# Moving the small projection's load to third place in each group of the gate's loads, and its products behind the group's first unit

## The chip, the cores and the metric

One core of a Trainium2 chip runs the kernel. The metric is the device time of one execution, in microseconds (us); the median of three runs is compared. A profile is one such execution, taken by the hardware profiler. Matrix products run on TensorE (PE; its weight loads are PEld), element-wise work on VectorE (DVE), ScalarE (ACT) and GpSimd (POOL), and SyncE (SP) issues the large weight loads from memory. Each engine works through its own program in order and meets the others at semaphores.

## The reference

Two transformer-like blocks in float32 follow each other on one sequence of 256 rows of 2048 values. The place that matters here is the end of the first block, after its MLP:

```python
        h = h + rms_norm(f, norm_mlp_post[i])
        h = h + jax.nn.sigmoid(h @ ple_gate[i]) * (p[i] @ ple_proj[i])
```

`ple_gate` is 2048 x 2048 (the gate) and `ple_proj` is 256 x 2048 (the small projection); `p` is 256 x 256. The result `h` then feeds the second block, whose first large product is with `w_in_2`.

## The kernel before, in words

**Units.** A weight matrix is read in column chunks of 512. A chunk of a 2048-row weight comes in four loads of 1 MB (rows 512 u to 512 u + 511, u = 0 to 3), each into one of four slots of the buffer `raw`. One such load with its products is a unit. For float32 accuracy the unit is split in two parts: ACT copies it to `whi` in fp32r (`hand_split`, L1112), DVE writes the rest, `raw - whi`, to `wlo` (`hand_low`, L1599), and PE then runs 24 matmuls of 128x512 for it, for two row halves b (`hand_unit`, L655 to L657). `whi` and `wlo` have two buffers each, so the split of a unit waits until PE is through with the unit two before it.

**The order of loads.** The first part of the program runs on one list that is written out by hand, `order` (L369 to L374), and turned into `HAND`. Entry n goes to slot n % 4. SP walks down that list and issues one load per entry (L535 to L558). Before load n it waits until entry n - 4, which lay in the same slot, has been used: for a split unit until DVE has written its `wlo` (`lo_ready`, L539), for a plain one, which PE reads straight from `raw`, until its products are done (`plain_used`, L541). SP is one queue: a load that waits holds up all loads behind it.

**The gate stage.** The gate has four chunks (i = 0 to 3) of four units (u = 0 to 3); the sixteen are the entries "gate". For each chunk there is one plain entry "pp" with the chunk's 512 columns of the small projection (0.5 MB, L547). Before the change each group of five entries reads pp, gate, gate, gate, gate. PE walks through the gate units (L912 to L927) and runs the chunk's small products behind unit u = 2: four float32 matmuls of 128x512 (L925), which the trace shows as eight. They write to PSUM banks 4 and 5 (even i) or 6 and 7 (odd i). Before them PE waits for the load (`raw_in`) and, for i of 2 and 3, for `gate_mul`, that is, for DVE to have read the bank's content of two chunks ago.

When a chunk's last unit is done, ACT takes the sigmoid of both halves (`sigmoids`, L1395), and DVE multiplies it with the small products (L2003, behind `plain_used`) and adds it to `h` (L2004, `gated`). ACT then forms row squares (L1345). After the last chunk DVE scales the rows, PE transposes them (L600, `turned("m2_00", ...)`), and the stage `in2_0` with 52 units begins (L931).

What sets the order around the change is therefore the list `order`, with the test in L916; nothing is scheduled by a program.

Of the kernel before, what the change touches and what calls it, by code (L numbers as in the profile page):

```python
# [91 lines left out]
def build(nc, I, out):  # L92
    ctx = ExitStack()
    with ctx:
# [261 lines left out]
        def laid(order):  # L356

            out_, done, s_, p_, a_ = [], {}, 0, 0, -2
            for r_, name in enumerate(order):
                ph = BY[name]  # L360
                k = done.get(name, 0)
                done[name] = k + 1
                if ph.split and k % UPC == 0:
                    a_ += 2
                out_.append(Unit(ph, k // UPC, k % UPC, r_, s_ if ph.split else None, None if ph.split else p_, a_))
                s_, p_ = s_ + (1 if ph.split else 0), p_ + (0 if ph.split else 1)
            return out_

        order = []  # L369
# [1 line left out]
            order += ["in1" if n < 36 else "in1g"] + (["mod0"] if n % 5 < 4 else [])  # L371
        order += ["in2_0c"] * 4 + ["cmp", "in2_0c"] * 4 + ["in2_0c"] * 40
        order += ["out1"] * 16 + ["in2_0c"] * 4 + ["mlp"] * 128
        order += (["pp"] + ["gate"] * 4) * 4 + ["in2_0"] * 52  # L374
        HAND = laid(order)
        SPLIT = [x for x in HAND if x.s is not None]

# [206 lines left out]
        def _(pe):  # L584
# [57 lines left out]
            def hand_unit(x, A):  # L642

                pe.wait_ge(lo_ready, x.s + 1)
                hi_, lo_ = A
                w = x.ph.width
                for b in range(TB):
                    a, bank = half(x, b)
                    if x.u == 0 and a >= 3:
                        pe.wait_ge(half_out, a - 2)  # L650
                    tt = slice(b * P, b * P + P)
                    dst = ps[:, bank, 0:w]
                    for k in range(UK):
                        kk = UK * x.u + k
                        mm(dst, hi_[:, kk, tt], whi[:, x.s % 2, k, 0:w], start=(kk == 0), stop=False)  # L655
                        mm(dst, hi_[:, kk, tt], wlo[:, x.s % 2, k, 0:w], start=False, stop=False)  # L656
                        ins = mm(dst, lo_[:, kk, tt], whi[:, x.s % 2, k, 0:w], start=False, stop=(kk == KT - 1))  # L657
                    if x.u == UPC - 1 and b == 0:
                        ins.then_inc(half_done, 1)
                ins.then_inc(unit_used, 1)  # L660
# [251 lines left out]
            for x in GATE:  # L912
                if x.i == 0:
                    pe.wait_ge(a_lo, PR["ple"]["t0"] + 2 * (x.u + 1))
                hand_unit(x, AY_)
                if x.u == 2:  # L916
                    y = PP[x.i]
                    pe.wait_ge(raw_in[y.slot], y.landed)
                    if x.i < 2:
                        pe.wait_ge(a_lo, PR["ple"]["t0"] + 8)  # L920
                    else:
                        pe.wait_ge(gate_mul, 2 * (x.i - 1))
                    for b in range(TB):
                        for k in range(2):
                            ins = mm(ps[:, 4 + 2 * (x.i % 2) + b, :], pT[:, k, b * P:b * P + P], raw[:, y.slot, k, :],  # L925
                                     start=(k == 0), stop=(k == 1))
                    ins.then_inc(plain_used, 1)  # L927
# [1472 lines left out]
```

## Time and profile before

| | |
|---|---|
| three runs | 3209.96, 3212.2 and 3218.76 us, median 3212.2 us |
| profiled execution | 3217.07 us, of which the profiled span is 3215.4 us (1.7 us lie around it) |
| PE busy in the span | 2860.1 us (89%) |
| DVE, ACT, POOL busy | 1653.0 us (51%), 1138.0 us (35%), 164.0 us (5%) |
| HBM | 183 GB/s mean over the span |
| gate stage, 1545.3 to 1697.5 us | PE busy 113.70 of 152.20 us |

The table is read as follows: PE has by far the most work, and the question in each stage is what ends its idle time. Times inside the span are counted from its start.

### The profile page before, as it was taken

Reading aid. Unit: us, or ns where it says so; the run is one execution under the profiler, and the core shown is the slowest. Engines: PE = TensorE matmul, PEld = TensorE weight load, DVE = VectorE, ACT = ScalarE, POOL = GpSimd, SP = SyncE. Lnnn points to the kernel's source line nnn. Section 1 sums busy time; section 2 is a strip of 40 time slices with the busy share of each in tenths; the row PEclk is TensorE's granted clock in tenths of the full one; section 3 lists DMA queues with packets and bytes.
Section 4 is the critical chain, followed back from the end, with each engine's and each line's share of the span. In section 5 each row is a group of like instructions: output and inputs, shape, how many; then the busy total and the mean of one; then the engine's idle time right before and its main releaser. Section 6 shows DMA issues by size and latency. Waiting matters only on the chain. (4 is left out here: it accounts for less than half of the span.)

```text
span 3215.4 us, 32172 instructions
## 1 busy us (share of the span) xinstructions
PE 2860.1 (89%) x13308; PEld 2243.1 (70%) x13308; DVE 1653.0 (51%) x1877; ACT 1138.0 (35%) x1389; POOL 164.0 (5%) x172
## 2 busy tenths in 40 slices
PE   5999899999999999999778998786599799996668
PEld 3777788888888888888556887432388678784356
DVE  3644556655545445454335444797533522346954
ACT  3452244444433333334223332353311411232433
POOL 0000100000000000011001000010000200000000
PEclk9998899999999999999888999899799899997779
DMA  6877464466656565655234666799232233464033
GB/s 227 278 248 238 139 232 148 151 237 195 206 185 195 184 196 183 196 183 188 71 144 166 211 221 222 296 348 362 101 137 92 99 124 119 155 217 171 1 135 131
DMA packets 284892, 589.27 MB, mean 183 GB/s; under 512 B 13522, under 2 KB 21562, under 8 KB 282192
## 3 DMA queue, kind: packets, MB, share of 16 engines
q1 hardware_dynamic: 261088, 512.13, 47.6%
q0 software_dynamic: 11552, 48.25, 4.0%
q10 hardware_dynamic: 12112, 26.91, 2.3%
q8 instruction: 102, 1.67, 0.2%
q14 instruction: 38, 0.31, 0.0%
HBM read 560.41 MB, written 26.84 MB: 183 GB/s over the span
## 5 line engine op out<-in xcount | busy, mean ns | idle before, releaser
L1599 DVE TENSOR_TENSOR wlo<-raw,whi 128x2048 fp32r<-128x2048 f32 x304 | 689.0, 2267 | 900.1 <-ACT whi L1112 899.8
L1112 ACT ACTIVATE whi<-raw 128x2048 fp32r<-128x2048 f32 x304 | 575.9, 1894 | 1139.3 <-PE ps L657 907.4
L655 PE MATMUL ps<-whi,ax_hi 128*128 128x512 f32 (+1 forms) x1376 | 540.4, 393 | 0.2 <-DVE wlo L1599 0.2
L657 PE MATMUL ps<-whi,ax_lo 128*128 128x512 f32 (+1 forms) x1376 | 535.0, 389 | 0.0
L656 PE MATMUL ps<-wlo,ax_hi 128*128 128x512 f32 (+1 forms) x1376 | 534.7, 389 | 0.0
L655 PE MATMUL ps<-whi,ay_hi 128*128 128x512 f32 x1056 | 423.2, 401 | 43.7 <-DVE wlo L1599 43.7
L656 PE MATMUL ps<-wlo,ay_hi 128*128 128x512 f32 x1056 | 417.0, 395 | 0.0
L657 PE MATMUL ps<-whi,ay_lo 128*128 128x512 f32 x1056 | 416.9, 395 | 0.0
L1592 DVE TENSOR_TENSOR wlo<-raw,whi 128x2048 fp32r<-128x2048 f32 x84 | 192.3, 2292 | 384.8 <-ACT whi L1104 384.4
L1104 ACT ACTIVATE whi<-raw 128x2048 fp32r<-128x2048 f32 x84 | 160.5, 1914 | 455.7 <-PE ps L616 450.3
L655 PEld LDWEIGHTS ps<-whi,ax_hi 128*128 128x128 f32 x1376 | 262.0, 190 | 76.5 <-issue 21.3
L657 PEld LDWEIGHTS ps<-whi,ax_lo 128*128 128x128 f32 x1376 | 261.9, 190 | 53.2
L656 PEld LDWEIGHTS ps<-wlo,ax_hi 128*128 128x128 f32 x1376 | 262.1, 190 | 51.0
L614 PE MATMUL ps<-whi,ax_hi 128*128 128x512 f32 x672 | 265.9, 396 | 32.1 <-DVE ay_lo L2203 13.6
L655 PEld LDWEIGHTS ps<-whi,ay_hi 128*128 128x128 f32 x1056 | 202.5, 192 | 88.7 <-DVE wlo L1599 37.3
L615 PE MATMUL ps<-wlo,ax_hi 128*128 128x512 f32 x672 | 263.9, 393 | 0.0
L616 PE MATMUL ps<-whi,ax_lo 128*128 128x512 f32 x672 | 263.7, 392 | 0.0
L657 PEld LDWEIGHTS ps<-whi,ay_lo 128*128 128x128 f32 x1056 | 201.9, 191 | 43.6
L656 PEld LDWEIGHTS ps<-wlo,ay_hi 128*128 128x128 f32 x1056 | 202.7, 192 | 41.1
L614 PEld LDWEIGHTS ps<-whi,ax_hi 128*128 128x128 f32 x672 | 127.9, 190 | 60.9 <-issue 27.0
L615 PEld LDWEIGHTS ps<-wlo,ax_hi 128*128 128x128 f32 x672 | 128.2, 191 | 26.4
L616 PEld LDWEIGHTS ps<-whi,ax_lo 128*128 128x128 f32 x672 | 127.7, 190 | 27.1
(366 smaller groups left out, 2805.1 us busy)
## 6 DMA issues: line engine op xcount, KB each, us to landing
raw<-in_w_in_dram SPq DMA_DIRECT2D x192, 1024.0 KB, 5.1
raw<-in_mlp_w_dram SPq DMA_DIRECT2D x128, 1024.0 KB, 5.3
raw<-in_w_mod_dram SPq DMA_DIRECT2D x96, 1024.0 KB, 8.4
raw<-in_w_out_dram SPq DMA_DIRECT2D x48, 1024.0 KB, 5.1
raw<-in_ple_gate_dram SPq DMA_DIRECT2D x16, 1024.0 KB, 5.6
z<-zst POOLq DMA_DIRECT2D x22, 512.0 KB, 4.4
z<-zsc POOLq DMA_DIRECT2D x13, 512.0 KB, 3.4
h<-in_x_dram POOLq DMA_DIRECT2D x2, 2048.0 KB, 10.9
```

The lines of the kernel that those rows point to most:

```text
L614: mm(dst, hi_[:, kk, tt], whi[:, u % 2, k, 0:width], start=(kk == 0), stop=False)
L615: mm(dst, hi_[:, kk, tt], wlo[:, u % 2, k, 0:width], start=False, stop=False)
L616: ins = mm(dst, lo_[:, kk, tt], whi[:, u % 2, k, 0:width], start=False, stop=(kk == KT - 1))
L655: mm(dst, hi_[:, kk, tt], whi[:, x.s % 2, k, 0:w], start=(kk == 0), stop=False)
L656: mm(dst, hi_[:, kk, tt], wlo[:, x.s % 2, k, 0:w], start=False, stop=False)
L657: ins = mm(dst, lo_[:, kk, tt], whi[:, x.s % 2, k, 0:w], start=False, stop=(kk == KT - 1))
L1104: A(whi[:, u % 2, :, 0:width], raw[:, u, :, 0:width], ACT.Copy).then_inc(hi_ready, 1)
L1112: A(whi[:, x.s % 2, :, 0:w], raw[:, x.slot, :, 0:w], ACT.Copy).then_inc(hi_ready, 1)
L1592: V.tensor_tensor(wlo[:, u % 2, :, 0:ph.width], raw[:, u, :, 0:ph.width], f32v(whi[:, u % 2, :, 0:ph.width]), ALU.subtract).then_inc(lo_re ...
L1599: V.tensor_tensor(wlo[:, x.s % 2, :, 0:w], raw[:, x.slot, :, 0:w], f32v(whi[:, x.s % 2, :, 0:w]), ALU.subtract).then_inc(lo_ready, 1)
```

## The change

In the list, pp moves from first to third place in its group. On PE, the small products of chunks 1 to 3 move from behind unit 2 to behind unit 0 of their chunk; those of chunk 0 stay behind unit 2. No instruction is added, removed or resized.

```diff
@@ -371,7 +371,7 @@
         order += ["out1"] * 16 + ["in2_0c"] * 4 + ["mlp"] * 128
-        order += (["pp"] + ["gate"] * 4) * 4 + ["in2_0"] * 52
+        order += ["gate", "gate", "pp", "gate", "gate"] * 4 + ["in2_0"] * 52
         HAND = laid(order)
@@ -913,7 +913,7 @@
                 hand_unit(x, AY_)
-                if x.u == 2:
+                if x.u == (0 if x.i else 2):
                     y = PP[x.i]
```

On SP's queue, this is where the loads of the MLP end and those of the gate begin; each row is a load with what it waits for, and `in_ple_proj` is the small projection.

```order
 L555 DMA raw<-in_mlp_w_dram 128x4x512 [waits lo_ready] x128
+L557 DMA raw<-in_ple_gate_dram 128x4x512 [waits lo_ready] x2
 L547 DMA raw<-in_ple_proj_dram 128x2x512 [waits lo_ready]
 L557 DMA raw<-in_ple_gate_dram 128x4x512 [waits lo_ready] x3
```

Two gate loads now stand ahead of the first pp. The same queue at the gate's end, where `in_w_in` are the loads of `in2_0`:

```order
 L557 DMA raw<-in_ple_gate_dram 128x4x512 [waits plain_used]
 L547 DMA raw<-in_ple_proj_dram 128x2x512 [waits lo_ready]
-L557 DMA raw<-in_ple_gate_dram 128x4x512 [waits lo_ready] x3
-L557 DMA raw<-in_ple_gate_dram 128x4x512 [waits plain_used]
-L557 DMA raw<-in_w_in_dram 128x4x512 [waits lo_ready] x52
+L557 DMA raw<-in_ple_gate_dram 128x4x512 [waits lo_ready] x2
+L557 DMA raw<-in_w_in_dram 128x4x512 [waits lo_ready]
+L557 DMA raw<-in_w_in_dram 128x4x512 [waits plain_used]
+L557 DMA raw<-in_w_in_dram 128x4x512 [waits lo_ready] x50
```

The load that waits for the small products (`plain_used`) was the same chunk's unit 3, the fourth entry behind pp; now it is the next chunk's unit 1, and behind the last pp the second load of `in2_0`.

On PE, chunk 1 of the gate before the change, from its first matmul; each row of L655 that waits is the first of a half or of a unit, and the rows between, all L655 to L657, are left out:

```order
L655 MATMUL ps<-whi,ay_hi 128x512 [waits half_out,lo_ready]
...
L655 MATMUL ps<-whi,ay_hi 128x512 [waits lo_ready]
...
L655 MATMUL ps<-whi,ay_hi 128x512 [waits lo_ready]
...
L925 MATMUL ps<-raw,zst 128x512 [waits a_lo,raw_in1]
L925 MATMUL ps<-raw,zst 128x512 x3
L655 MATMUL ps<-whi,ay_hi 128x512 [waits lo_ready]
```

And after it:

```order
L655 MATMUL ps<-whi,ay_hi 128x512 [waits half_out,lo_ready]
...
L655 MATMUL ps<-whi,ay_hi 128x512 [waits half_out]
...
L925 MATMUL ps<-raw,zst 128x512 [waits a_lo,raw_in3]
L925 MATMUL ps<-raw,zst 128x512 x3
L655 MATMUL ps<-whi,ay_hi 128x512 [waits lo_ready]
```

The small products stood behind three units, now behind one, and they read slot 3 in place of slot 1. On DVE, ACT and POOL the order of instructions is the same before and after.

## Rows read from the trace of the kernel before

**Rows 1.** The page: span, and busy time, share and instructions by engine.

```profile
span 3215.4 us, 32172 instructions
...
PE 2860.1 (89%) x13308; PEld 2243.1 (70%) x13308; DVE 1653.0 (51%) x1877; ACT 1138.0 (35%) x1389; POOL 164.0 (5%) x172
```

**Rows 2.** Windows: the MLP stage, the gate stage, and six us behind a pause.

```profile
core 0: us, PE busy (x) PEld busy (x) DVE busy (x) ACT busy (x) POOL busy (x), PEclk, DMA share, GB/s
800.00:1500.00 700.00, 700.00 (x3172) 581.28 (x3172) 358.47 (x230) 268.22 (x183) 43.31 (x39) 1.00 0.60 192
1545.30:1697.50 152.20, 113.70 (x417) 86.02 (x415) 44.72 (x31) 37.49 (x34) 0.00 (x0) 0.86 0.37 135
1613.00:1619.00 6.00, 5.78 (x14) 4.52 (x15) 2.46 (x2) 2.16 (x2) 0.00 (x0) 0.50 0.88 324
```

**Rows 3.** Waits of the engines, 1525 to 1725 us: total, times, longest.

```profile
ACT whi L1112 <- DMA raw<-in_ple_gate_dram: 77.6, 7, 17.5
...
PE ps L655 <- DVE wlo L1599: 37.8, 4, 9.5
```

**Rows 4.** Waits of SP's queue, 1500 to 1725 us: total, times, longest.

```profile
SPq L557 <- PE ps L925: 126.1, 4, 42.4
```

**Rows 5.** Timeline: start, duration, engine, instruction, [idle before it <- what ended it].

```profile
1562.51 3.59 PE L925 MATMUL ps<-raw,zst 128*128 128x512 f32 x8
1575.65 0.76 PE L655 MATMUL ps<-whi,ay_hi 128*128 128x512 f32 x1 [9.55 <-DVE wlo L1599]
...
1600.25 3.59 PE L925 MATMUL ps<-raw,zst 128*128 128x512 f32 x8
...
1603.88 0.37 SPq L557 DMA_DIRECT2D raw<-in_ple_gate_dram  x1
...
1608.93 1.91 ACT L1112 ACTIVATE whi<-raw 128x2048 fp32r<-128x2048 f32 x1 [17.38 <-DMA raw<-in_ple_gate_dram]
...
1610.88 2.29 DVE L1599 TENSOR_TENSOR wlo<-raw,whi 128x2048 fp32r<-128x2048 f32 x1 [17.00 <-ACT whi L1112]
...
1613.22 0.79 PE L655 MATMUL ps<-whi,ay_hi 128*128 128x512 f32 x1 [9.38 <-DVE wlo L1599]
...
1619.22 0.40 PE L657 MATMUL ps<-whi,ay_lo 128*128 128x512 f32 x1
...
1696.46 0.39 PE L657 MATMUL ps<-whi,ay_lo 128*128 128x512 f32 x1
1704.55 1.73 PE L600 MATMUL ps<-eye,yb 128*128 128x128 f32 x7 [7.70 <-issue]
```

**Rows 6.** Timeline of ACT in the MLP stage, two units running.

```profile
1508.16 1.92 ACT L1112 ACTIVATE whi<-raw 128x2048 fp32r<-128x2048 f32 x1 [3.52 <-PE ps L657]
1513.60 1.92 ACT L1112 ACTIVATE whi<-raw 128x2048 fp32r<-128x2048 f32 x1 [3.52 <-PE ps L657]
```

**Rows 7.** Timeline of DVE: `wlo` of the gate's units 0 and 2.

```profile
1526.42 2.29 DVE L1599 TENSOR_TENSOR wlo<-raw,whi 128x2048 fp32r<-128x2048 f32 x1 [3.14 <-ACT whi L1112]
...
1553.83 2.29 DVE L1599 TENSOR_TENSOR wlo<-raw,whi 128x2048 fp32r<-128x2048 f32 x1 [7.16 <-ACT whi L1112]
```

**Rows 8.** Timeline behind chunk 0: second sigmoid, split of chunk 1's unit 1, gating.

```profile
1584.13 0.60 ACT L1395 ACTIVATE zst<-ps 128x512 f32<-128x512 f32 x1 [2.39 <-PE ps L657]
...
1586.56 2.29 DVE L1599 TENSOR_TENSOR wlo<-raw,whi 128x2048 fp32r<-128x2048 f32 x1 [6.50 <-ACT whi L1112]
...
1590.81 0.69 DVE L2004 TENSOR_TENSOR h<-h,zst 128x512 f32<-128x512 f32 x1
```

**Rows 9.** Loads of the gate, then of the small projection: issue to landing, min/median/max.

```profile
DMA to landing us min/median/max: 5.0/7.2/11.8
...
DMA to landing us min/median/max: 3.6/6.4/6.4
```

**Rows 10.** Timeline of PE in the first stage: two matmuls behind plain products.

```profile
100.67 0.50 PE L655 MATMUL ps<-whi,ax_hi 128*128 128x512 f32 x1
101.00 0.39 PE L656 MATMUL ps<-wlo,ax_hi 128*128 128x512 f32 x1
```

## Prediction

> **What bounds the kernel now.** I read the page first. PE is busy for 89% of the span, DVE for 51% [rows 1]. So what matters is where PE stands still, and for what. The windows by stage say where. In the 700 us of the MLP stage PE is busy all the time at the full clock (PEclk 1.00); in the gate stage it is busy for 113.70 of 152.20 us, and the clock is at 0.86 [rows 2]. That is the stage of the change.
>
> The waits say for what. PE waited four times for DVE's `wlo`, 37.8 us in all; but ACT, which feeds DVE, waited for the gate's loads [rows 3]. Behind ACT stands SP's queue: four loads of the gate waited 126.1 us for L925, the small products [rows 4]. So PE waits for something that waits for PE.
>
> The timeline shows one such round. The eight rows of L925 begin at 1600.25. They start 0.43 us apart ((3.59 - 0.59) / 7, the last lasting 0.59), so PE is through with starting them at 1600.25 + 8 x 0.43 = 1603.69. SP issues a gate load at 1603.88; ACT begins `whi` at 1608.93, DVE `wlo` at 1610.88, and PE goes on at 1613.22 [rows 5]. The code names this load: pp of chunk i is entry 5i, unit 3 of the same chunk is entry 5i + 4, so they share a slot. Unit 3 can't be loaded before the small products are done, and these stand directly in front of unit 3. Nothing covers the load (about 5 us), `whi` (1.91) and `wlo` (2.29). That happens once per chunk, four times.
>
> The pause costs more than its idle time. Behind it the granted clock is 0.50, the lower level of 1.2 GHz [rows 2]: the first 14 matmuls of the unit, from 1613.22 to 1619.22, take 6.00 us [rows 5]. At the full clock a unit of 24 matmuls takes 1513.60 - 1508.16 = 5.44 us [rows 6], or 0.227 us each, so these 14 would take 3.17 us. The lower clock costs 2.83 us per pause.
>
> **The change, part by part.** No instruction is added or removed; order alone changes.
>
> *The load of unit 3.* Unit 3 of chunk i (entry 5i + 4) now follows unit 0 of its chunk (entry 5i) in the slot, and waits for unit 0's `wlo`. For chunk 0 that is written at 1526.42 + 2.29 = 1528.71 [rows 7], so the load lands some 5 us later, near 1534. Its `whi` then waits only for PE to finish unit 1. `wlo` of unit 2 ends at 1553.83 + 2.29 = 1556.12 [rows 7]. Unit 1 ends near 1557.1, which is the start of the products, 1562.51, less one unit. So `wlo` of unit 3 is ready at about 1557.1 + 1.9 + 2.3 + 0.2 = 1561.5. PE is through with the products at 1562.51 + 3.44 = 1565.95: no pause, with 4.4 us to spare.
>
> *The load that now waits for the products.* It is unit 1 of the next chunk. For chunk 1 it is issued at 1565.95 + about 0.2, as before at 1603.88 [rows 5]. Between that and its use stand unit 3 of chunk 0, unit 0 of chunk 1 and the small products of chunk 1: PE wants it at 1565.95 + 5.44 + 5.44 + 3.44 = 1580.3. With a landing in 5.0 to 7.2 us [rows 9], it is there by 1573.4. ACT takes it up behind the second sigmoid of chunk 0, and its `wlo` ends (1586.56 + 2.29) - 1584.13 = 4.7 us after that sigmoid begins [rows 8], here at about 1571.4 + 4.7 = 1576.1. Spare: 4.2 us. In chunks 2 and 3 the products stand behind unit 0, three units earlier than before, and the load has four units and the next products in front of it. Its cover grows to 25 us.
>
> *The load of pp.* For chunk 1 it is queued behind that same unit 1, so it is issued at about 1566.6 and lands within 6.4 us [rows 9], at 1573.0. PE reaches the products at 1565.95 + 2 x 5.44 = 1576.8. This is the tightest new wait, with 3.8 us to spare. In chunks 2 and 3 SP isn't held.
>
> *The products' other wait, and who stands behind it.* For chunks 2 and 3 PE waits for `gate_mul`, the gating of two chunks ago; behind PE's wait stands everything. Gating of chunk 0 ended at 1590.81 + 0.69 = 1591.50, 7.4 us after the second sigmoid began [rows 8]; in the new time that is 1579, and the products of chunk 2 come at 1571.4 + 5 x 5.44 + 3.44 = 1602. It costs nothing. DVE's wait for the small products in `gated` becomes shorter. Its work of a chunk (4 x 2.29 and 4 x 0.7, 12 us) lies in 25 us of PE's.
>
> *Loads of the next stage.* The first of `in2_0` move up with the queue. Their use waits for the row scaling and the transposes behind the last gate unit, the 7.70 us of idle time at 1704.55 [rows 5]. That tail hangs on the last unit's end, by ACT and DVE work that doesn't move, so it comes earlier as a whole and costs what it did.
>
> *Small cost.* Behind plain products the first matmul of a unit takes 0.33 us to the next one (100.67 to 101.00) in place of 0.23 [rows 10]. The trace of before has no gate unit directly behind L925, since a pause follows each; this is the nearest row. I take 0.10 us, four times; its bounds are 0 and the whole 0.50 us of that matmul, 2 us in all.
>
> **The sum.** PE is through with the first products at 1565.95 in both kernels. Before, its last gate matmul ends at 1696.46 + 0.39 = 1696.85 [rows 5]: 130.90 us. After: 13 units x 5.44 = 70.72; three groups of products x 3.44 = 10.32; 4 x 0.10 = 0.40; and 0.16 for the last matmul beyond its start distance. Together 81.60 us. The difference is 49.3 us. As a cross-check, four pauses are 37.8 us by the waits [rows 3] and about 38.5 us by the start times, since the wait is counted from the last matmul's end; four restarts cost 4 x 2.83 = 11.3; that is 49.8, less 0.4.
>
> Nothing downstream has a time of its own, so the span should be 3215.4 - 49.3 = 3166.1 us and that execution 3217.07 - 49.3 = 3167.8 us. The profiled execution was 4.9 us above the median of the runs, 3212.2 us; from the median the forecast is **3162.9 us**, 1.5% faster. The size of such differences between runs sets +-5 us about it.
>
> **The clock, by the trace and by a page.** In the row, 14 matmuls are slow behind the pause shown, and without the pause PE enters each unit as it does in the MLP stage, at 1.00. So all 11.3 us return. The Trainium skill (TensorE: Matmul & The Clock Gate, Part 1: The HAM clock gate) says that the throttled state is the default and that activity releases it; here the clock is 0.50 behind 9.38 us of idle time and 1.00 through the MLP stage, which agrees. The same section reports that the number of slow matmuls at a start varies from run to run of one kernel, and names 6, 11 and 14. With 6, as an estimate from that page, only 4 x 6 x 0.20 = 4.8 us would return, and the time would be 3169.4 us.
>
> **Rivals.**
> - *Late loads at chunk 1.* SP releases unit 1, pp, and units 2 and 3 of chunk 1 in one go at 1566, 3.5 MB. For: before, such a burst stretched landings to 11.8 us [rows 9]. Against: that is the last of a burst; the first in the queue, which is the one in need, landed in 5. If unit 1 took 11.8 us, `wlo` would be ready at 1566.1 + 11.8 + 4.4 = 1582.3, 2.0 us late, and pp, 0.5 us behind it in the queue, 1.6 us late for the products in front; a whole chunk's pause again would be 12.4 us (9.5 + 2.8). 3165 to 3175 us.
> - *The clock doesn't return.* The idle time goes, but the stage still has slow stretches as long as before. Gain 38.5 - 0.4 = 38.1: 3174 us. For: the stage starts behind idle time, and DVE, ACT and DMA are now busy closer together. Against: the MLP stage has 192 GB/s and stays at 1.00 [rows 2].
> - *Slower.* The one mechanism with a price that large is the granted clock staying at its lower level through the stage, now that PE has no pause in it. A slow matmul costs 0.43 - 0.23 = 0.20 us; 13 units x 24 x 0.20 = 62 us against 49.3 gained: 3225 us. It decides once 247 of the 312 matmuls are slow. Against: 700 us without a pause at 1.00 [rows 2].
> - *No change.* The gain is given back further on: the tail or `in2_0` would have to wait for something that doesn't come earlier, such as a load or a store on POOL's queue. Then 3212 us. I find no such thing: every load of `in2_0` hangs on the gate's own progress.
>
> **How the numbers follow.** The forecast as worked out, 3157 to 3169 us, gets 0.82; late loads 0.05; the clock not returned 0.06; given back 0.04; slower 0.03. From 3155 to 3175 us the range holds the first with the spread of the runs and most of the next two, about 8 to 9 in 10. What a measurement of this kernel can tell from no change is about 0.3%, 10 us. All gains above lie beyond it: faster 0.93, within it 0.04, slower 0.03.
>
> **What would show it.** In the profile of the changed kernel: no wait of PE for DVE in the gate stage, where four stood; PE busy throughout from about 1545 to 1647.5 us, with PEclk 1.00 behind the first few us; the small products of chunk 1 near 1576.8, with no idle time before them; ACT's waits for the gate's loads nearly gone; the last gate matmul ending near 1647.5, and the transposes of L600 near 1655.3. A wait of PE for DMA before L925 at chunk 1 would show the first rival, PEclk below 1.00 within the stage the second or third. The prediction is wrong if a pause stays with another releaser, or if the stage shrinks by 49 us and the span does not.

## The result

The changed kernel takes 3167.05 us (median of 4 runs, 3162.89 to 3169.92); the kernel before, now with 4 runs, 3215.48 us (3209.96 to 3219.36). The ratio is 0.985, with a 95% interval of 0.9829 to 0.9871: 1.5% faster, 48.4 us by the medians. Forecast were 3162.9 us and a gain of 49.3 us. Of the 4.2 us between the forecast and the time, 3.3 us are the base: the median of before that the forecast started from was 3212.2 us, and one more run moved it to 3215.48.

The page of the changed kernel, with the rows that answer to [rows 1], and from its second part the granted clock (one digit for each 40th of the span, in tenths of full speed). The last line is the clock on the page of the kernel before:

```profile
span 3164.4 us, 32172 instructions
...
PE 2850.4 (90%) x13308; PEld 2235.1 (71%) x13308; DVE 1652.6 (52%) x1877; ACT 1137.7 (36%) x1389; POOL 163.9 (5%) x172
...
PEclk9999899999999999999999998898799899997779
...
PEclk9998899999999999999888999899799899997779
```

The instructions are as many as before; the span is 51.0 us shorter. PE's busy time falls by 9.7 us although it does the same work: matmuls behind a pause had lasted longer. The three digits 8 in the middle of the clock of before are the gate stage; they are 9 now. Next its waits from 1520 to 1725 us (total, times, longest), to be read against [rows 3]:

```profile
PE ps L600 <- DVE h L1927: 8.0, 3, 4.1
PE ps L600 <- issue: 7.7, 1, 7.7
PE ps L600 <- DVE yb L2016: 4.8, 2, 2.6
```

The wait of L655 for `wlo`, 37.8 us in four pieces, is gone. What is left are the waits of the transposes at both ends of the stage. ACT, which waited 77.6 us for the gate's loads, waits for none; its splits now wait for PE to free a buffer (1525 to 1725 us):

```profile
ACT whi L1112 <- PE ps L657: 87.9, 22, 7.0
```

SP's queue, 1500 to 1725 us, against [rows 4]:

```profile
SPq L557 <- DVE wlo L1599: 167.7, 26, 26.3
SPq L557 <- PE ps L925: 37.5, 4, 26.3
```

There still are four waits of a load for the small products, but neither ACT nor PE waits for a load behind them. The timeline of PE, with the small products of chunks 0, 1 and 3 and the transposes behind the stage, against [rows 5]:

```profile
1559.11 3.59 PE L925 MATMUL ps<-raw,zst 128*128 128x512 f32 x8
...
1573.44 3.59 PE L925 MATMUL ps<-raw,zst 128*128 128x512 f32 x8
1576.47 0.79 PE L655 MATMUL ps<-whi,ay_hi 128*128 128x512 f32 x1
1577.10 0.40 PE L656 MATMUL ps<-wlo,ay_hi 128*128 128x512 f32 x1
...
1623.85 3.59 PE L925 MATMUL ps<-raw,zst 128*128 128x512 f32 x8
...
1651.48 3.65 PE L600 MATMUL ps<-eye,yb 128*128 128x128 f32 x16 [7.70 <-issue]
```

From the first small product to the end of the last gate matmul it is 1651.48 - 7.70 - 1559.11 = 84.67 us; before, 1696.85 - 1562.51 = 134.34 us. The windows of the same stretch and of the one in front of it, in the columns of [rows 2]:

```profile
1541.85:1559.10 17.25, 17.25 (x73) 14.16 (x72) 5.79 (x4) 4.43 (x3) 0.00 (x0) 0.94 0.00 1
1559.10:1643.80 84.70, 84.68 (x345) 64.46 (x343) 38.62 (x27) 32.46 (x29) 0.00 (x0) 1.00 0.60 205
```

PE is busy in all of it, at a granted clock of 1.00, while 205 GB/s arrive.

### The profile page after: what moved, and what is told of

Same layout as the page of the kernel before. It is cut to its first block and busy times, and to the rows that moved or that the text cites. A ratio compares the mean times of both kernels' runs of the same rounds, so it can differ in the third digit from the quotient of the medians.

```text
span 3164.4 us, 32172 instructions
## 1 busy us (share of the span) xinstructions
PE 2850.4 (90%) x13308; PEld 2235.1 (71%) x13308; DVE 1652.6 (52%) x1877; ACT 1137.7 (36%) x1389; POOL 163.9 (5%) x172
## 3 DMA queue, kind: packets, MB, share of 16 engines
q1 hardware_dynamic: 261088, 512.13, 48.4%
## 5 line engine op out<-in xcount | busy, mean ns | idle before, releaser
L655 PE MATMUL ps<-whi,ax_hi 128*128 128x512 f32 (+1 forms) x1376 | 539.9, 392 | 0.9 <-DVE wlo L1599 0.9
L657 PE MATMUL ps<-whi,ax_lo 128*128 128x512 f32 (+1 forms) x1376 | 534.4, 388 | 0.0
L655 PE MATMUL ps<-whi,ay_hi 128*128 128x512 f32 x1056 | 419.9, 398 | 6.0 <-DVE wlo L1599 6.0
L657 PE MATMUL ps<-whi,ay_lo 128*128 128x512 f32 x1056 | 413.9, 392 | 0.0
L655 PEld LDWEIGHTS ps<-whi,ax_hi 128*128 128x128 f32 x1376 | 260.3, 189 | 75.2 <-issue 20.8
L657 PEld LDWEIGHTS ps<-whi,ax_lo 128*128 128x128 f32 x1376 | 260.3, 189 | 53.6
L655 PEld LDWEIGHTS ps<-whi,ay_hi 128*128 128x128 f32 x1056 | 200.2, 190 | 47.9 <-DVE wlo L1599 6.7
L657 PEld LDWEIGHTS ps<-whi,ay_lo 128*128 128x128 f32 x1056 | 199.5, 189 | 42.4
```

## The experiments

One distance serves to compare all kernels: from the end of the MLP's last matmul (the start of the first L600 less the idle time before it) to the first matmul of `in2_0`. It holds the whole gate stage and its lead-in and tail. The column "runs" is the ratio to the kernel before, with its interval; each ratio is to runs of the kernel before that were taken together with it (their medians lie between 3212.3 and 3215.5 us), so kernels are best compared by the ratios and the stages.

| kernel | stage, us | against the changed kernel | runs |
|---|---|---|---|
| before | 1529.82 to 1716.63: 186.8 | +49.6 | |
| changed | 1526.36 to 1663.57: 137.2 | | 0.985 (0.9829 to 0.9871) |
| only the list | 1527.09 to 1664.20: 137.1 | -0.1 | 0.9844 (0.983 to 0.9857) |
| only the products | 1527.95 to 1676.33: 148.4 | +11.2 | 0.9884 (0.9869 to 0.99) |
| before, pauses filled | 1526.61 to 1703.22: 176.6 | +39.4 | 0.9962 (0.9948 to 0.9975) |
| one unit of cover | 1524.57 to 1683.86: 159.3 | +22.1 | 0.9918 (0.9901 to 0.9935) |
| all behind unit 0 | 1524.58 to 1661.85: 137.3 | +0.1 | 0.9841 (0.9826 to 0.9856) |
| changed, ends filled | 1529.06 to 1662.50: 133.4 | -3.8 | 0.9827 (0.9813 to 0.984) |

The theory: what made the pauses is a slot, shared by the small projection's columns and a unit that PE needs soon behind their products. The pause is the length of the chain (load, `whi`, `wlo`), less the PE work that stands between. The rivals are that both halves of the change are needed, and that the slow restart behind a pause comes from the loads that land then and not from the clock.

### Only the list

```diff
-        order += (["pp"] + ["gate"] * 4) * 4 + ["in2_0"] * 52
+        order += ["gate", "gate", "pp", "gate", "gate"] * 4 + ["in2_0"] * 52
```

L916 stays at `x.u == 2`. Expected:

> Only the list of loads is changed (pp third in its group); the small products stay behind unit 2 in all chunks. Slot theory: what ends a pause is how much PE work stands between the small products and the unit whose load waits for them. Here unit 3 and the next chunk's unit 0 stand between, 2 x 5.44 = 10.9 us, against a chain of 9.5 us (load, whi, wlo) that the second sigmoid lengthens to about 10.2 us. No pause, some 0.7 us to spare: as fast as the changed kernel, 1.5% under the kernel before, the gate stage within 1 us of the changed kernel's. Rival, the products must move too: without their move the pause only goes from unit 3 to the next chunk's unit 1, three or four pauses stay, and the time is near that of before (3203 to 3216 us).

The runs took 3164.99 us (5 runs), and the stage is the changed kernel's to 0.1 us. PE from 1541.8 to 1652.5 us has one wait, that of the tail:

```profile
PE ps L600 <- issue: 7.7, 1, 7.7
```

How near the next pause was is on DVE's timeline, with `wlo` of unit 1 in chunks 1 and 2:

```profile
1571.24 2.29 DVE L1599 TENSOR_TENSOR wlo<-raw,whi 128x2048 fp32r<-128x2048 f32 x1 [7.03 <-ACT whi L1112]
...
1596.45 2.29 DVE L1599 TENSOR_TENSOR wlo<-raw,whi 128x2048 fp32r<-128x2048 f32 x1 [7.03 <-ACT whi L1112]
```

PE's own:

```profile
1584.93 3.59 PE L925 MATMUL ps<-raw,zst 128*128 128x512 f32 x8
```

The second is ready at 1598.74; PE wants it at 1584.93 + 3.44 + 10.88 = 1599.25. It was 0.5 us in time. This margin is not set by the load. The rows are SP's issue of this load, its time from issue to landing, and ACT's second sigmoid of chunk 1 with the split of this unit behind it:

```profile
1588.56 0.37 SPq L557 DMA_DIRECT2D raw<-in_ple_gate_dram  x1
...
DMA to landing us min/median/max: 5.1/5.1/5.1
...
1594.02 0.60 ACT L1395 ACTIVATE zst<-ps 128x512 f32<-128x512 f32 x1 [2.12 <-PE ps L657]
1594.51 1.91 ACT L1112 ACTIVATE whi<-raw 128x2048 fp32r<-128x2048 f32 x1
```

The load had landed at 1593.7, 0.8 us before ACT came to it: the split stands behind the sigmoid, and the sigmoid waits for PE's last matmul of the chunk. The kernel before has the same 0.5 us at chunk 1, where this load is not the one that waits for the products: `wlo` is ready at 1586.56 + 2.29 = 1588.85 [rows 8], and PE wants it two units before the products of 1600.25 [rows 5], at 1589.37. So here the load could have come some 0.8 + 0.5 = 1.3 us later before PE waited. The move on PE brings no time of its own; it widens these margins. The rival falls.

### Only the products

```diff
-                if x.u == 2:
+                if x.u == (0 if x.i else 2):
```

The list stays as before. Expected:

> Only the place of the products is changed (behind unit 0 in chunks 1 to 3); pp stays first in its group. Slot theory: in chunks 1 to 3 units 1 and 2, 10.9 us of PE work, now cover the load of unit 3, whose chain is 9.5 us, so three pauses go; chunk 0 keeps its pause. One pause costs 9.7 us idle and 2.8 us of slow clock: 12.5 us slower than the changed kernel, about 37 us (1.15%) faster than before. Rival, the order of the loads is what matters: the pauses stay and the time is that of before.

The runs took 3178.64 us (4 runs), 11.6 us above the changed kernel's; the stage is 11.2 us longer, where 12.5 us had been expected. The waits of PE, 1535 to 1660 us:

```profile
PE ps L655 <- DVE wlo L1599: 9.6, 1, 9.6
```

And the place of that wait:

```profile
1559.78 3.59 PE L925 MATMUL ps<-raw,zst 128*128 128x512 f32 x8
1572.97 0.77 PE L655 MATMUL ps<-whi,ay_hi 128*128 128x512 f32 x1 [9.60 <-DVE wlo L1599]
```

Three of four pauses are gone with the order of loads untouched; the one left is chunk 0's, whose products stand behind unit 2. From its first matmul behind the pause to the next small products (at 1586.21) it is 13.24 us for two units, which at the full clock take 10.88: this restart cost 2.4 us, and not 2.8. Another 0.9 us of the difference to the expectation is in front of the pause, where the first gate matmuls ran at the full clock sooner than in the changed kernel (16.69 us from the first gate matmul to the first small product, 17.60 there). Each half of the change removes pauses alone, since each puts two units of PE work between products and load. It is the distance that counts, not which of the two is moved.

### The kernel before with its pauses filled

```diff
                     ins.then_inc(plain_used, 1)
+                    for _ in range(40):
+                        mm(ps[:, 3, :], ay_hi[:, 0, 0:P], ay_hi[:, 0:2, :].rearrange("p k t -> p (k t)"), start=True, stop=True)
```

Expected:

> The kernel before, with 40 matmuls whose result nobody reads put behind each of the four small products (fp32r, 128x512, from ay_hi into the unused PSUM bank 3). They take 40 x 0.227 = 9.1 us of the 9.4 to 9.5 us that PE is idle and delay nothing. Clock theory: the granted clock stays at 1.00, the 14 slow matmuls behind each pause run at the full clock, and each chunk gets 2.8 us shorter: 11.3 us (0.35%) faster than before, the pauses before unit 3 still ending at the same distance from the products. Rival: the restart is slow for another reason (the loads that land then, 324 GB/s): the first matmuls still start 0.43 us apart and the time is that of before.

The runs took 3203.47 us (5 runs), 0.38% under the kernel before. One round on PE (the fillers are L929):

```profile
1594.22 3.59 PE L925 MATMUL ps<-raw,zst 128*128 128x512 f32 x8
1597.25 9.64 PE L929 MATMUL ps<-ay_hi 128*128 128x512 f32 x40
1607.38 0.50 PE L655 MATMUL ps<-whi,ay_hi 128*128 128x512 f32 x1 [0.48 <-DVE wlo L1601]
1607.71 0.40 PE L656 MATMUL ps<-wlo,ay_hi 128*128 128x512 f32 x1
1607.95 0.39 PE L657 MATMUL ps<-whi,ay_lo 128*128 128x512 f32 x1
```

And the window around it, then the six us behind the pause, to be read against the last line of [rows 2]:

```profile
1594.00:1620.00 26.00, 25.52 (x106) 19.48 (x105) 8.93 (x7) 9.41 (x10) 0.00 (x0) 1.00 0.50 182
1607.00:1613.00 6.00, 5.62 (x25) 4.67 (x26) 2.61 (x2) 2.52 (x2) 0.00 (x0) 1.00 0.91 334
```

The unit begins 1607.38 - (1594.22 + 3.44) = 9.72 us behind the products, as it did (9.53 to 9.70 us); its matmuls follow at 0.23 us but for the first, where they had 0.43. The granted clock is 1.00 while 334 GB/s land, against 0.50 and 324 GB/s. So the slow restart was the clock and not the loads. The stage is 186.81 - 176.61 = 10.2 us shorter, where 11.3 us had been expected. Of the 1.1 us between them 0.15 us are the units that begin later, and 0.95 us their matmuls: between a unit's first matmul and the next small products (or the stage's end) the four stretches last 0.10, 0.13, 0.58 and 0.14 us longer than units of 5.44 us; what slowed them is open. Work that nobody reads made this kernel faster, by 0.38%, because it kept the clock up.

### One unit of cover

```diff
-        order += (["pp"] + ["gate"] * 4) * 4 + ["in2_0"] * 52
+        order += ["gate", "pp", "gate", "gate", "gate"] * 4 + ["in2_0"] * 52
```

The products stay behind unit 2, so only unit 3 stands between them and the next chunk's unit 0, whose load waits. Expected:

> pp stands second in its group, the products behind unit 2. The load that waits for the products is now the next chunk's unit 0, with only unit 3 (5.44 us) in between. Slot theory: a pause of 9.5 - 5.4 = 4.1 us before unit 0 of chunks 1, 2 and 3, none before unit 3; behind the last chunk the waiting load is the next stage's and its delay hides in the row scaling. 12.3 us slower than the changed kernel if the clock stays up, up to 20.8 us (3 x 2.8 more) if it falls behind such a pause. Rival, any order in which unit 3 doesn't share the slot does as well: as fast as the changed kernel.

The runs took 3186.64 us (4 runs). PE's waits, 1535 to 1660 us:

```profile
PE ps L655 <- DVE wlo L1599: 12.1, 3, 4.1
```

Its timeline: unit 0 of chunks 2 and 3, and the tail:

```profile
1601.37 0.80 PE L655 MATMUL ps<-whi,ay_hi 128*128 128x512 f32 x1 [4.00 <-DVE wlo L1599]
...
1633.78 0.50 PE L655 MATMUL ps<-whi,ay_hi 128*128 128x512 f32 x1 [4.00 <-DVE wlo L1599]
...
1671.77 3.65 PE L600 MATMUL ps<-eye,yb 128*128 128x128 f32 x16 [10.89 <-issue]
```

And the window behind the pause of chunk 2:

```profile
1602.00:1608.00 6.00, 6.00 (x16) 4.67 (x15) 4.29 (x5) 2.84 (x5) 0.00 (x0) 0.54 0.73 269
```

Three pauses of 4.0 to 4.1 us, as worked out from 9.5 - 5.4. The clock falls behind them too (at chunk 2 the first matmul takes 0.80 us; at chunk 3 it still takes 0.50). The stage is 22.1 us longer than the changed kernel's, more than the 20.8 us expected at most. 3.2 us of it were not expected at all: the tail's idle time is 10.89 us in place of 7.70. The rest is 22.1 - 12.1 - 3.2 = 6.8 us, and nearly all of it, 6.3 us, is slow matmuls behind the pauses: the three units up to the next small products last 1.52, 3.04 and 1.73 us longer than at the full clock, where 2.8 us each had been taken at most. I had taken the late load of the next stage to be hidden in the row scaling. It isn't, and ACT's waits, 1640 to 1680 us, show why:

```profile
ACT whi L1112 <- DMA raw<-in_w_in_dram: 12.1, 1, 12.1
```

In ACT's program the split of `in2_0`'s first unit stands in front of the last chunk's sigmoids. ACT waits for a load that nobody needs yet, and the sigmoids, on which the tail hangs, wait behind it.

### All small products behind unit 0

```diff
-                if x.u == (0 if x.i else 2):
+                if x.u == 0:
```

Expected:

> The changed kernel, with chunk 0's small products behind unit 0 too. Slot theory: no pause in either, the load that waits for these products is released 10.9 us earlier, which nobody needs: the same time within 0.3% and the gate stage within 1 us. Rival: chunk 0's products stand behind unit 2 for a reason (their load or the last of ay_lo comes late), and PE waits for 1 to 5 us before them.

The runs took 3164.42 us (4 runs), the stage 137.3 us. PE has no wait between the transposes at the two ends; the exception for chunk 0 neither helps nor hurts.

### The changed kernel with both ends filled

What was still slow around the stage in the changed kernel is the clock at its ends:

```profile
1526.00:1542.00 16.00, 8.02 (x35) 6.95 (x34) 13.10 (x19) 7.73 (x14) 2.50 (x2) 0.74 0.39 132
1643.80:1665.00 21.20, 8.67 (x36) 7.61 (x37) 18.26 (x30) 10.56 (x19) 6.79 (x6) 0.56 0.30 98
```

```diff
+            def fill(src, n):
+                for _ in range(n):
+                    mm(ps[:, 3, :], src[:, 0, 0:P], src[:, 0:2, :].rearrange("p k t -> p (k t)"), start=True, stop=True)
             for i in range(4):
+                fill(ax_hi, (16, 0, 12, 0)[i])
                 turned("ple", i, 4)
...
+            fill(ay_hi, 16)
             pe.wait_ge(gate_mul, 8)
+            fill(ay_hi, 14)
             for i in range(4):
+                fill(ay_hi, (0, 0, 8, 10)[i])
                 turned("m2_00", i, 8)
```

Expected:

> The changed kernel, with matmuls whose result nobody reads in the idle time around the gate stage: 16 and 12 before the transposes that lead into it, 30 behind its last unit and 8 and 10 between the transposes behind it. Clock theory: the granted clock stays up at both ends of the stage; some six slow matmuls at each end (0.2 us each) and the slow transposes go, 2 to 5 us less than the changed kernel, which its runs can hardly tell. Rival: the fillers delay the transposes, and the stage gets longer.

The runs took 3160.66 us (5 runs). Its windows over both ends:

```profile
1525.00:1545.00 20.00, 16.82 (x88) 13.43 (x88) 16.89 (x22) 8.54 (x15) 2.55 (x2) 1.00 0.43 146
1643.00:1665.00 22.00, 18.24 (x95) 14.68 (x95) 19.46 (x31) 10.85 (x19) 7.16 (x6) 1.00 0.29 96
```

The clock is at 1.00 in both, and the stage is 3.8 us shorter: 1.4 us up to the first gate matmul, 1.2 us from there to the first small product, and 1.2 us behind the last gate matmul. So small a difference shows in the runs only side by side, so both kernels were measured again on one chip:

> The changed kernel once more, unedited, beside the next one on one chip. Expected ratio to the kernel before 0.984 to 0.986.

> The changed kernel with the fillers around the gate stage once more. The traces put it 3.8 us ahead of the changed kernel between the end of the MLP and the first product of in2_0; if that reaches the end of the program the runs are 0.12% shorter than the changed kernel's on the same chip. Rival: it is lost again further on, and the two are the same within 0.05%.

The changed kernel took 3167.01 us (ratio 0.9862, 0.9846 to 0.9877), the filled one 3160.11 us (0.9841, 0.9827 to 0.9854); their stages are 137.1 and 133.4 us. The medians are 6.9 us apart, and 6.4 us the first time, but the intervals still overlap, and the two profiled spans differ by only 0.6 us (3159.1 and 3158.5 us). I take the filled kernel for the fastest of those here: by 3.7 to 3.8 us in the stage, which two pairs of traces show, while the runs do not show clearly how much of it reaches the end of the program.

## Why the prediction was right

**The pauses.** Forecast were no waits of PE for `wlo` in the stage. There are none. That the slot was the cause is shown from three sides: by the list alone, by the products alone, and by the pause of 4.0 us with one unit of cover. The rule pause = 9.5 us less the PE work between held at none, one (5.4 us) and two units (10.9 us). The places came as forecast too: the profiled execution was 3.46 us ahead at the end of the MLP (1526.36 against 1529.82), and with this added, chunk 1's small products begin at 1576.9 (forecast 1576.8), the last gate matmul ends at 1647.2 (1647.5), and the transposes begin at 1654.9 (1655.3).

**The clock.** Taken as 4 x 2.83 = 11.3 us, from one pause. The other pauses of the kernel before bear it out: from the first matmul behind a pause to the next small products (in the last chunk to the stage's end) the four stretches are 2.84, 2.84, 2.82 and 2.74 us longer than units of 5.44 us, 11.24 us in all. Filling the pauses gave 10.2 us. In the changed kernel it came back in full: from first small product to last gate matmul the gain was 134.34 - 84.67 = 49.67 us, where 49.3 was forecast; the four pauses by start times (9.70, 9.53, 9.54 and 9.69 us) are 38.46 of it, and the rest is 11.2 us. By the number of slow matmuls at a start that the Trainium skill names as the lowest (6; TensorE: Matmul & The Clock Gate, Part 1: The HAM clock gate) it would have been 4.8 us, as an estimate; the 14 slow matmuls of [rows 5] gave the better price. The forecast's rival in which the clock stays low in the stage fell: 1.00 over 84.7 us.

**The small cost** of 0.10 us behind each group of products was not there. The eighth product of chunk 1 starts at 1573.44 + 7 x 0.43 = 1576.45, the unit's first matmul right behind it at 1576.47, and its second at 1577.10, as if the unit had begun at 1573.44 + 8 x 0.43 = 1576.88. Without this term the sum is 49.7 us, the measured value.

**The new waits.** For unit 1 of chunk 1, 4.2 us to spare was forecast. That number holds only if the load lands before ACT is through with the second sigmoid; with the 7.2 us that the prediction allows it would not have, and its own numbers give 1573.4 + 4.4 = 1577.8, 2.5 us to spare. The load (issued at 1562.74) took 5.1 us. Its `wlo` ended at 1570.63 + 2.29 = 1572.92 (the first row below), and PE wanted it at 1573.44 + 3.44 = 1576.88: 4.0 us.

```profile
1570.63 2.29 DVE L1599 TENSOR_TENSOR wlo<-raw,whi 128x2048 fp32r<-128x2048 f32 x1 [7.03 <-ACT whi L1112]
```

For the small projection's load of chunk 1, 3.8 us was forecast. SP issued it at 1563.15, and the longest landing of the four was 6.5 us (issue to landing, min, median, max, against [rows 9]):

```profile
DMA to landing us min/median/max: 3.9/5.7/6.5
```

So it was there by 1569.7, 3.8 us before PE began at 1573.44. The rival of late loads thus fell by its own test: the first load of the burst took 5.1 us, the last 10.8 us, and no engine waited for it. In two details the prediction is wrong without effect. In chunks 1 to 3 the small products stand two units earlier than before, not three; the four units of cover that it counts are right. And SP is held in chunks 2 and 3 as well: it issued chunk 2's waiting load only at 1577.1, behind the small products of chunk 1, and the small projection's load behind that at 1577.96. This one landed 5.7 us later, 15 us before its use at 1598.65.

**What surrounds the stage.** The forecast was that the tail costs what it did and nothing is given back. Its idle time is 7.70 us, as before, and from the last gate matmul's end to the first matmul of `in2_0` it is 19.79 us, 19.78 before. Outside the stage the profiled executions differ by small amounts: -3.5 us ahead of it, where the program is the same, and +2.1 us behind it. These sum with -49.6 to the 51.0 us of the spans. They say nothing on the change: two profiles of the changed kernel have spans of 3164.4 and 3159.1 us, with stages of 137.2 and 137.1 us.

**What the prediction had too loosely.** It said that the use of the next stage's first loads waits for the row scaling and the transposes. That holds for PE but not for ACT, which takes the split of the first of them ahead of the last chunk's sigmoids. For the changed kernel it cost nothing because that load was early; in the run with one unit of cover it was late, and the tail grew by 3.2 us.

## What to carry to other kernels

Where loads share a ring of slots, look for each load's predecessor in its slot, and count the work of the bound engine between the release of the one and the use of the other: that must exceed the whole chain behind the load, not the load alone. A gap beyond it is worth nothing more, so the cheapest edit that gets there is enough. A load that may be late in one queue is harmless only if no engine has an instruction for it ahead of work that others need. And a pause on TensorE is to be priced with its slow restart, here 2.4 to 2.8 us on top of 9.4 to 9.6 us, and 1.5 to 3.0 us on top of 4.0 us.

## What the runs showed of the hardware

- A pause of 4.0 us of TensorE was enough to bring the granted clock down: in the run with one unit of cover the next 14 matmuls of chunk 2 started 0.43 us apart, as many as behind a pause of 9.4 us in the kernel before. Behind pauses as long the slow restart was shorter at chunk 1 (1.5 us lost, 3.0 us at chunk 2), and at chunk 3 (1.7 us lost) the first matmuls were at full speed and the slow ones came after.
- 40 matmuls into an unused PSUM bank kept the granted clock at 1.00, with 0.4 to 0.5 us of idle time left, while 334 GB/s landed; without them it was 0.50 at 324 GB/s. The units behind lost 0.95 us in all four places, where they had lost 11.24 us.
- In the trace the unit behind a group of float32 products starts its first matmul at 1576.47, 0.02 us after the start of the last product, where the products start 0.43 us apart; its second matmul, at 1577.10, stands where it would if nothing had been lost in the change from one kind to the other.
